# Short-convolution stage: where the output projection's operand is kept, and when each part of it is split

## What is computed

```python
def short_conv_mixer(h, w_in, conv_w, w_out):
    b_gate, c_gate, xin = jnp.split(h @ w_in, 3, axis=-1)
    y = causal_depthwise_conv_2(c_gate * xin, conv_w)
    return (b_gate * y) @ w_out
```

## Time and profile before

| | |
|---|---|
| median of three runs | 3400.12 us (3398.66 to 3400.54) |
| span of the profiled execution | 3394.2 us (no separate time of this execution is recorded) |
| TensorE busy | 3265.1 us, 96% of the span |
| VectorE busy | 1883.5 us, 55% |
| ScalarE busy | 1584.3 us, 47% |
| mean TensorE clock granted | 0.984 |

### The profile page before, as it was taken

One profiled execution on the slowest core, in us unless ns is written; L12 is line 12 of the kernel. 1 busy time (PEld: TensorE's weight loads), 2 busy tenths in 40 slices (PEclk: granted clock), 3 DMA queues, 4 the chain that ended last, 5 costly groups with the idle time before them and its releaser, 6 DMA issues.

```text
span 3394.2 us, 49319 instructions
## 1 busy us (share of the span) xinstructions
PE 3265.1 (96%) x19406; PEld 2766.6 (82%) x19406; DVE 1883.5 (55%) x2067; ACT 1584.3 (47%) x1921; POOL 194.0 (6%) x185
## 2 busy tenths in 40 slices
PE   8997799999999999989999999999999999999899
PEld 7887788888778888978888888888777888898787
DVE  4566655654564556755554555555655555575554
ACT  4446344544444545644444434444445435464543
POOL 0000000100000300120000000000320000003000
PEclk9999899999999999999999999999989999999999
DMA  6543255455255555415555546555522655552354
GB/s 218 189 128 90 75 201 179 157 197 186 81 180 185 174 185 163 150 39 166 189 179 188 177 144 202 189 178 190 160 90 75 192 179 188 189 154 68 108 190 136
DMA packets 423770, 535.46 MB, mean 158 GB/s; under 512 B 21122, under 2 KB 370798, under 8 KB 423632
## 3 DMA queue, kind: packets, MB, share of 16 engines
q1 hardware_dynamic: 421840, 528.76, 47.9%
q0 software_dynamic: 1792, 4.72, 0.6%
HBM read 532.36 MB, written 1.05 MB: 157 GB/s over the span
## 4 chain that ended last, share of the span: by engine, by line
PE 91%; DVE 4%; ACT 4%; issue 1%; DMA 0%; DVEq 0%; ACTq 0%
PE banks L133 24%; PE banks L135 24%; PE banks L134 24%; PE banks L130 3%; PE banks L132 3%; PE banks L131 3%; PE banks L318 2%; PE banks L1745 1%; DVE w_lo L114 1%; ACT w_hi L106 1%; PE banks L253 1%; ACT xT_hi L191 1%; PE banks L1128 1%; PE banks L1140 1%; ACT xn L174 0%
## 5 line engine op out<-in xcount | busy, mean ns | idle before, releaser
L114 DVE TENSOR_TENSOR w_lo<-raw,w_hi 128x2048 fp32r<-128x2048 f32 x514 | 1182.8, 2306 | 649.0 <-ACT w_hi L106 649.0
L106 ACT ACTIVATE w_hi<-raw 128x2048 fp32r<-128x2048 f32 x514 | 982.2, 1916 | 537.9 <-PE banks L135 443.8
L133 PE MATMUL banks<-w_hi,xT_hi 128*128 128x512 f32 (+1 forms) x2672 | 1030.0, 385 | 60.8 <-issue 33.6
L135 PE MATMUL banks<-w_hi,xT_lo 128*128 128x512 f32 (+1 forms) x2672 | 1016.5, 380 | 0.0
L134 PE MATMUL banks<-w_lo,xT_hi 128*128 128x512 f32 (+1 forms) x2672 | 1014.7, 380 | 0.0
L133 PEld LDWEIGHTS banks<-w_hi,xT_hi 128*128 128x128 f32 x2672 | 507.0, 190 | 159.2 <-issue 39.2
L135 PEld LDWEIGHTS banks<-w_hi,xT_lo 128*128 128x128 f32 x2672 | 506.7, 190 | 96.0
L134 PEld LDWEIGHTS banks<-w_lo,xT_hi 128*128 128x128 f32 x2672 | 507.4, 190 | 90.2
L133 PE MATMUL banks<-w_hi,hidT_hi 128*128 128x512 f32 x1056 | 411.9, 390 | 0.0
L135 PE MATMUL banks<-w_hi,hidT_lo 128*128 128x512 f32 x1056 | 411.1, 389 | 0.0
L134 PE MATMUL banks<-w_lo,hidT_hi 128*128 128x512 f32 x1056 | 410.9, 389 | 0.0
(11 more groups left out here) (434 smaller groups left out, 2466.9 us busy)
## 6 DMA issues: line engine op xcount, KB each, us to landing
raw<-ffn_w_gate_up SPq DMA_DIRECT2D x352, 512.0 KB
raw<-ffn_w_down SPq DMA_DIRECT2D x264, 512.0 KB
raw<-ffn_w_gate SPq DMA_DIRECT2D x88, 512.0 KB
raw<-ffn_w_up SPq DMA_DIRECT2D x88, 512.0 KB
raw<-gdn_w_in SPq DMA_DIRECT2D x64, 512.0 KB
raw<-sc_w_in SPq DMA_DIRECT2D x24, 512.0 KB
raw<-rg_w_in SPq DMA_DIRECT2D x32, 336.0 KB
raw<-nsa_w_in SPq DMA_DIRECT2D x20, 512.0 KB
```

Source lines behind the costliest of these rows:

```text
L106: c.nc.scalar.activation(c.w_hi[r][:], c.raw[r][:], ACT.Copy).then_inc(c.sem("w_hi_split"), 1)
L114: c.nc.vector.tensor_tensor(c.w_lo[r][:], c.raw[r][:], c.w_hi[r][:].bitcast(F32), ALU.subtract).then_inc(c.sem("w_lo_split"), 1)
L133: mm(out, x_hi, w_hi, start=start, stop=False)
L135: return mm(out, x_lo, w_hi, start=False, stop=stop)
```

## The change

The operand of `w_out` goes to blocks 8 to 15 of `xT_hi` and `xT_lo`. ScalarE no longer waits for the last slab of `w_b` before it writes them; each high part follows the weight split of its `w_b` step, and each low part likewise on VectorE. TensorE waits for two low parts ahead of the first slab of `w_out`'s first step, and for all four ahead of the second slab.

```diff
-def pe_project(c, pe, pr, after=None, ready=None, norm=None, operand=None):
+def pe_project(c, pe, pr, after=None, ready=None, norm=None, operand=None, operand_home=0):
...
-            x_hi, x_lo = operand(k) if operand else (c.xT_hi[0:pr.rows, k, x], c.xT_lo[0:pr.rows, k, x])
+            x_hi, x_lo = operand(k) if operand else (c.xT_hi[0:pr.rows, operand_home + k, x],
+                                                    c.xT_lo[0:pr.rows, operand_home + k, x])
...
     pe_project(c, pe, w_b)
-    pe.wait_ge(c.sem("sc_gated_lo"), w_b.steps)
-    pe_project(c, pe, w_out)
+    pe_project(c, pe, w_out, ready=lambda q: pe.wait_ge(c.sem("sc_gated_lo"), 2 * q + 2), operand_home=KD)
...
     act_project(c, act, w_x, after=first_tap)
-    act_project(c, act, w_b)
-    act.wait_ge(c.sem("slab_used"), w_b.slab + w_b.steps)
-    for s in range(w_b.steps):
+
+    def gated_hi(s):
         act.wait_ge(c.sem("projection_read"), w_b.step + s + 1)
-        pair = slice(2 * s, 2 * s + 2)
-        scalar.activation(c.xT_hi[:, pair, :], v.gated[:, pair, :], ACT.Copy).then_inc(c.sem("sc_gated_hi"), 1)
+        scalar.activation(c.xT_hi[:, KD + 2 * s:KD + 2 * s + 2, :], v.gated[:, 2 * s:2 * s + 2, :], ACT.Copy
+                          ).then_inc(c.sem("sc_gated_hi"), 1)
+
+    act_project(c, act, w_b, after=gated_hi)
     act_project(c, act, w_out)
...
+
+    def gated_lo(s):
+        dve.wait_ge(c.sem("sc_gated_hi"), s + 1)
+        home = slice(KD + 2 * s, KD + 2 * s + 2)
+        vector.tensor_tensor(c.xT_lo[:, home, :], v.gated[:, 2 * s:2 * s + 2, :], c.xT_hi[:, home, :].bitcast(F32),
+                             ALU.subtract).then_inc(c.sem("sc_gated_lo"), 1)
+
     dve_project(c, dve, w_b, lambda s, view: vector.tensor_tensor(
-        v.gated[:, 2 * s:2 * s + 2, :], v.y[:, 2 * s:2 * s + 2, :], view, ALU.mult))
-    for s in range(w_b.steps):
-        dve.wait_ge(c.sem("sc_gated_hi"), s + 1)
-        pair = slice(2 * s, 2 * s + 2)
-        vector.tensor_tensor(c.xT_lo[:, pair, :], v.gated[:, pair, :], c.xT_hi[:, pair, :].bitcast(F32), ALU.subtract
-                             ).then_inc(c.sem("sc_gated_lo"), 1)
+        v.gated[:, 2 * s:2 * s + 2, :], v.y[:, 2 * s:2 * s + 2, :], view, ALU.mult), after=gated_lo)
     dve_project(c, dve, w_out, dve_add_to_h(c, w_out))
```

## The result

| | before | changed | |
|---|---|---|---|
| median of 15 runs each | 3399.93 us | 3391.17 us | ratio 0.9977, 95% interval 0.9969 to 0.9984 |
| span of the profiled execution | 3394.2 us | 3387.4 us | 6.8 us |

The forecast was 3391.5 us, in a range of 3388.5 to 3394.5. The kernel is faster by 8.8 us between the medians (7.9 between the means, 3399.1 and 3391.2), but the two profiled executions differ by only 6.8 us. That difference is the first thing to explain. Part of it is which executions were profiled: in every run on record the time is 1.7 to 1.8 us above the core's span, so the profiled execution of the kernel before took about 3396.0 us and that of the changed kernel 3389.09, both near the low end of their runs.

The account below looks back on a forecast made before the run. TensorE was taken as the bound (91% of the last chain), with a 6.8 us wait before `w_out`. Removing 6.95 us idle and 1.65 us half clock takes the span from 3394.2 to 3385.6; plus 5.9 gives 3391.5 us, range 3388.5 to 3394.5.

Parts of the forecast that it names:

- The start of `w_out`: First matmul of `w_out` comes one distance, 0.12 us, behind the last of `w_b`, at 1996.14; 6.95 us of idle removed.
- the three conditions of the first slab: Before `w_out`'s first matmul: two low parts, the split of slab 4 and a free PSUM bank, all claimed long done.
- The clock's 1.65 us: `w_out`'s first step takes 10.88 us instead of 12.53, since without the idle time TensorE stays at 2.4 GHz.
- The second slab: The added wait at the second slab of `w_out`'s first step: stall taken as zero, at most 0.3 us.
- My margin of 0.06 us: At the second slab, the last low part is seen at 2001.29, the weight load that waits is due at 2001.35.
- The moved splits cost nothing: Per `w_b` step, ScalarE's extra 0.54 us and VectorE's extra 0.62 us fit into idle times of 3.84 and 1.46 us.
- The sum of the stage: From `w_b`'s end through `w_out`'s first step, idle and clock terms together save 8.60 us, 6.95 + 1.65.
- The later loads ... move with everything else. None is late.: Behind the first step of `w_out`, weight loads released by VectorE shift along with the work and cause no new wait.
- The step that failed: The whole 8.60 us saved around `w_out` comes off the end of the span, 3394.2 to 3385.6.
- rival (a): Idle goes, but 1.65 us is lost to half clock: saving 6.95, time 3393.2; chance 0.11 shared with a partial rival.
- The 5.9 us that I kept between span and time: Whole kernel: profiled span lay 5.9 us below the runs' median, 3400.12; added to the forecast span 3385.6 for the time.
- such changes are small in sum: Later half-clock changes over the whole kernel add up to little, since three earlier runs lay within 1.9 us.

Follow-up runs that it names:

- the wait was filled: The kernel before with 40 extra matmuls, results unused, put into TensorE's wait ahead of `w_out`; median 3399.91 us, ratio 0.9999.
- the late low part: The changed kernel with two extra VectorE subtractions ahead of the last low part, making it 1.2 us later; one run, 3393.64 us.
- The two halves of the change: Against the kernel before: early splits with one wait for all low parts (median 3401.07 us); waits per slab with late splits (medians 3403.14 and 3401.57 us).
- slab waits alone: The kernel before with old blocks and late splits kept, but TensorE waiting per slab of `w_out`; medians 3403.14 and 3401.57 us.

## Why the prediction was right, point by point

- **The start of `w_out`.** Forecast 1996.14, 0.12 us behind the last matmul of `w_b`; measured 0.12 us behind it. None of the three conditions of the first slab was late.
- **The clock's 1.65 us.** Right in kind and nearly in size: 1.51 us when the wait was filled.
- **The second slab.** No stall, as taken. My margin of 0.06 us was too small: the late low part measured 0.31 us to the matmul's start and 0.17 us to the end of the step. I had taken a late weight load to cost its full lateness, and it cost 0.11 us.
- **The moved splits cost nothing.** VectorE's idle time before the reading fell from 1.46 to 0.86 us (about 0.8 forecast), and ScalarE's before its split from 3.84 to 3.32; TensorE's pace in `w_b` did not change.
- **The sum of the stage.** Forecast 8.60 us, measured 8.57, in both profiles. First reading at 2007.32 (forecast 2007.2), norm at 2018.86 (2018.8).
- **"The later loads ... move with everything else. None is late."** This held for loads and waits: the list of waits behind the stage is the same to 0.2 us a line.
- **The step that failed** is in the sum, that a saving of 8.60 us in the stage goes to the end of the span in full. It did not: 1.7 us is given back in the sparse-attention stage, in both profiles. This is rival (a) with a loss of the size that it named, though not by a further fall of the clock but by one that lasts 3.3 us longer, and it gives a saving of 6.9 us by the profiles. The runs say 7.9 +- 0.5 us by the means, 8.8 by the medians of the first 15. The 1 us between profiles and means is not explained and is twice the error.
- **That the time was met to 0.3 us is luck in part.** The forecast took 8.60 us off 3400.12, the median of three runs, and the mean of all 86 is 3399.2, 0.9 us lower. Too high a start and too large a saving cancelled. The 5.9 us that I kept between span and time are no constant either: 1.7 to 1.8 us of them are in every run, the other 4.1 us come from the execution that was profiled. Added to the measured span, 3387.4, they would give 3393.3.
- **"such changes are small in sum"**, said against (a) from three runs within 1.9 us, was a wrong use of that number. The 86 runs spread over 8.4 us, and what the profiles show of that spread lies ahead of the stage. It says nothing of a loss behind the stage that is the same in every profiled execution.
- The Trainium skill, "TensorE: Matmul & The Clock Gate", section "Part 1: The HAM clock gate", has the gate's window run freely and not start with the kernel, so that the point of a change varies from run to run. The traces agree for the first 930 us. Behind them they do not: the profiles with the same program keep step to 0.1 us up to the stage, and behind it each kernel profiled twice or more repeats within 0.15 us. What brings every execution into the same step by 930 us, no run here shows.

The two halves of the change are worth little apart (stage -1.0 and -0.6 us) and 8.6 us together. With one wait for all parts, TensorE sits through the last weight split whatever is ready early; with late splits, the first two parts are behind that split too. Only together does the first slab's work (5.4 us) cover the 5.1 us until the last low part.

## What to carry to other kernels

When an operand is made in parts behind other work, look at which part each consumer needs first and give it a home that the previous reader does not block; early parts and fine waits gain only together. Price the idle time of TensorE with the matmuls at half clock that follow it (6.95 and 1.65 us here). Differences of a few microseconds in a kernel like this are best read part by part in the profile, since the clock in untouched stages moved the total by 1.6 to 3.8 us, enough to turn a small real saving into a loss.

## What the runs showed of the hardware

- Each of the five kernels that were profiled twice or more takes the same time behind the stage (before 1367.5 to 1367.6 us three times; slab waits alone 1371.3 and 1371.4), while the part ahead of it varies by up to 3 us for one and the same kernel, all of it ahead of 930 us.
- A shift of a few microseconds changes how long TensorE stays at half clock in a stage that the change does not touch: 20.5 us before and 23.8 us in the changed kernel, with 1.5 us lost.
- A shorter wait left more matmuls at half clock: behind a wait of 6.8 us the stage lost 1.65 us to them; when the wait was 1.8 us shorter, the stage got only 1.0 us shorter.
- At full clock, a matmul of 512 columns that had waited mostly cost 0.11 us beyond its wait (0.34 us to the next instead of 0.23: the two of the experiments, and four in the profile of before behind waits of 1.4 to 3.9 us). Behind waits of 0.45 us it was 0.08 us (0.31), and behind one of 3.1 us, at 367.4 us, nothing.
